# Normalisation factors held one per token on partitions, and the rotations of the grouped heads at another place

## The reference, cut to what matters

```python
def rmsnorm(x, g):
    y = xf * lax.rsqrt(jnp.mean(xf * xf, axis=-1, keepdims=True) + NORM_EPS)
    return (y * g).astype(x.dtype)
...
        x_gq = rope2d(rmsnorm(x_gq, gqa_q_norm_g[i]))
        x_gk = rope2d(rmsnorm(x_gk, gqa_k_norm_g[i]))
...
    s = jnp.einsum('bqhgd,bkhd->bhgqk', qblk, k) * scale
    p = jax.nn.softmax(s, axis=-1)
...
    od = (o1 - lam * o2)[:, :, :, 0, :]
    od = rmsnorm(od, subln_g) * (1.0 - lambda_init)
    og = attend(gq.reshape(B, S, GQA_KV_HEADS, GQA_GROUP, HEAD_DIM), gk, gv)
    o = jnp.concatenate([od.reshape(B, S, DIFF_WIDTH), og.reshape(B, S, GQA_WIDTH)], axis=-1)
    return o @ w_out
```

## Time and profile before

| | |
|---|---|
| median of 3 runs | 1671.21 us (1670.35 to 1672.07) |
| span of the profiled execution | 1662.7 us |
| time around the span, by the median | 8.5 us |
| PE, DVE, ACT, POOL busy | 84%, 57%, 37%, 18% of the span |
| moved by DMA | 572 MB, 344 GB/s in the mean |
| stage of the projections | about 37 to 143 us |
| attention and output of the first tile | about 143 to 196 us |
| expert loop with the gathers | from about 214 us |

### The profile page before, as it was taken

One profiled execution on the slowest core, in us unless ns is written; L12 is line 12 of the kernel. 1 busy time (PEld: TensorE's weight loads), 2 busy tenths in 40 slices (PEclk: granted clock), 3 DMA queues, 4 the chain that ended last, 5 costly groups with the idle time before them and its releaser, 6 DMA issues.

```text
span 1662.7 us, 21762 instructions
## 1 busy us (share of the span) xinstructions
PE 1397.3 (84%) x8112; PEld 860.6 (52%) x8112; DVE 951.8 (57%) x2127; ACT 623.5 (37%) x1464; POOL 300.1 (18%) x277
## 2 busy tenths in 40 slices
PE   5997877777776666677676999999999999999997
PEld 4884744543432323233322899898745454545443
DVE  4989588666668677677765788675431212121213
ACT  3334558354445444344443337544421111111111
POOL 0000034334435443444441000000000000000000
PEclk8999999989999888888977999999999999999999
DMA  9772189999999999999998534343799999999996
GB/s 395 283 270 97 39 346 398 395 427 418 417 427 413 421 426 399 427 423 425 427 424 339 193 133 150 123 178 136 316 385 427 426 427 427 428 427 427 426 427 273
DMA packets 80015, 572.09 MB, mean 344 GB/s; under 512 B 9136, under 2 KB 9392, under 8 KB 11184
## 3 DMA queue, kind: packets, MB, share of 16 engines
q1 hardware_dynamic: 40608, 284.55, 42.1%
q0 software_dynamic: 39312, 286.28, 41.8%
HBM read 569.75 MB, written 1.05 MB: 343 GB/s over the span
## 4 chain that ended last, share of the span: by engine, by line
PE 48%; DMA 17%; DVE 14%; SPq 11%; ACT 5%; issue 3%; POOL 1%; POOLq 0%; DVEq 0%; ACTq 0%
DMA big<-in_peer_dram,misc 13%; PE bank L1889 11%; SPq L518 11%; PE bank L1454 7%; DVE big L2241 5%; PE bank L1678 4%; PE bank L1399 2%; PE bank L1876 2%; PE bank L1636 2%; PE bank L1640 2%; DMA big<-in_moe_far_up_dram 2%; PE bank L1632 1%; POOL big L626 1%; DMA ring<-in_first_dram 1%; PE bank L1208 1%
## 5 line engine op out<-in xcount | busy, mean ns | idle before, releaser
L1454 PE MATMUL bank<-big 128*64 128x512 f32 x1024 | 302.4, 720 | 190.6 <-ACT big L821 189.9
L626 POOL DMA_INDIRECT big<-in_peer_dram,misc x256 | 290.7, 1135 | 472.6 <-PE bank L1454 338.2
L1454 PEld LDWEIGHTS bank<-big 128*64 128x64 f32 x1024 | 70.3, 153 | 352.8 <-ACT big L821 245.3
L2241 DVE SCALAR_TENSOR_TENSOR big<-big 128x1024 f32<-128x1024 f32 x128 | 156.0, 1226 | 98.9 <-DMA big<-in_peer_dram,misc 98.0
L2241 DVE SCALAR_TENSOR_TENSOR big<-big,misc 128x1024 f32<-128x1024 f32 x128 | 155.3, 1224 | 77.3 <-DMA big<-in_peer_dram,misc 76.2
L815 ACT ACTIVATE misc<-misc 128x1 f32<-128x1 f32 x256 | 51.5, 201 | 265.0 <-DVE big L2241 252.7
L1889 PE MATMUL bank<-big 128*64 128x512 f32 x640 | 140.2, 593 | 4.0 <-DMA big<-in_moe_far_up_dram 2.6
L2678 DVE SCALAR_TENSOR_TENSOR big_parts<-bank,misc,big_parts 128x512 fp32r<-128x512 f32 x32 | 22.5, 746 | 160.1 <-ACT big_parts L1099 160.1
L2668 DVE TENSOR_TENSOR misc<-misc,bank 128x512 f32<-128x512 f32 x16 | 11.0, 689 | 164.3 <-PE bank L1889 164.3
L1889 PEld LDWEIGHTS bank<-big 128*64 128x64 f32 x640 | 45.8, 137 | 95.8 <-issue 89.3
L821 ACT ACTIVATE big<-misc 128x64 f32<-128x64 f32 x256 | 89.0, 348 | 8.4
(11 more groups left out here) (485 smaller groups left out, 2574.0 us busy)
## 6 DMA issues: line engine op xcount, KB each, us to landing
big<-in_moe_down_dram SPq DMA_DIRECT2D x40, 1024.0 KB, 23.6
big<-in_moe_gate_dram SPq DMA_DIRECT2D x40, 1024.0 KB, 25.3
ring<-in_second_dram SPq DMA_DIRECT2D x36, 1024.0 KB
ring<-in_first_dram SPq DMA_DIRECT2D x33, 1024.0 KB
big<-in_moe_far_up_dram SPq DMA_DIRECT2D x20, 1024.0 KB, 22.6
big<-in_moe_up_dram SPq DMA_DIRECT2D x20, 1024.0 KB, 21.0
misc<-in_mod_rest_dram POOLq DMA_DIRECT2D x16, 1024.0 KB, 5.2
ring<-in_moe_gate_dram SPq DMA_DIRECT2D x12, 1024.0 KB, 21.5
```

The costliest lines, as they stand in the source:

```text
L626: pool.indirect_dma_start(out=gathered[b % GATHERS], out_offset=None, in_=t["peer"], in_offset=bass.IndirectOffsetOnAxis(ap=rows[:, b % 32 ...
L1454: last = nc.tensor.matmul(bank[2 * tt + half][HALF * g:HALF * (g + 1), :], diag[:, b % DIAGS, :], gathered[b % GATHERS][:, a:a + 512], sta ...
L2241: dve.scalar_tensor_tensor(u, u, 1.0, x_pairs[b // (BLOCKS // 2)][:, b % 2, :], ALU.mult, ALU.mult, accum_out=dots[:, b % 32:b % 32 + 1]). ...
```

## The change

The factors of the three norms are no longer spread over 128 x 512 elements, but held with tokens on partitions.

- **Grouped queries.** ACT squares a unit straight from PSUM and then copies it with the gain as scale. The sum over a head is eight products with the squares as the stationary operand and two columns of ones moving, the result 16 columns. The root is of the sum plus 64 times epsilon, which folds the factor of the scores' scale in. The inverse isn't multiplied into the queries: it is the scale of the exponential and a factor of the negative maximum. Queries are rotated without it.
- **Grouped keys.** Four products give sums per token (8 columns), then root and inverse; eight products of the inverse, repeated over 64 columns, with the identity spread it over bank 6, and DVE multiplies from PSUM.
- **Differential heads.** Four products with one column, root and inverse of 4 columns; then spread_od, four products with the identity, and DVE multiplies from PSUM. In out_first the fourth column block isn't begun early any more, and the blocks' banks change places.
- **Order.** The key sum stands after gq0 and not after gq1; the spread after gq2, behind a wait for the inverse; the query sums and the rotations of gk, gq0 and gq1 after gv; those of gq2 and gq3 after dv0. On DVE the rotations stand before pairs 10 and 11 instead of behind all pairs, and the multiplication of the keys behind remainder 9.

```diff
-        csT = small[:, 24:40]
+        eps_head = small[:, 1:2]
+        head_inv = small[:, 24:40].rearrange("p (t u r) -> p t u r", t=TT, u=4)
+        key_inv = small[:, 106:114].rearrange("p (t r) -> p t r", r=2)
+        od_inv = small[:, 114:118]
...
-            return bank[((0, 1, 4, 6), (2, 3, 5, 6))[tt][n % 4]][:, 0:P]
+            return bank[((1, 4, 6, 0), (2, 3, 5, 6))[tt][n % 4]][:, 0:P]
...
-                act.activation(dst[what](i), src, ACT.Copy).then_inc(S("win_taken"), 1)
+                if what == "gq":
+                    act.activation(sq[:, 2 + i // 2, (i % 2) * T:(i % 2 + 1) * T], src, ACT.Square).then_inc(S("sqg_ready"), 1)
+                    act.activation(dst[what](i), src, ACT.Copy, scale=v("gq_g")).then_inc(S("win_taken"), 1)
+                else:
+                    act.activation(dst[what](i), src, ACT.Copy).then_inc(S("win_taken"), 1)
...
-                if what == "gq":
-                    act.wait_ge(S("win_taken"), n + 1)
-                    act.activation(sq[:, 2 + i // 2, (i % 2) * T:(i % 2 + 1) * T], gqT[:, i, :], ACT.Square).then_inc(S("sqg_ready"), 1)
-                if n in (11, 14, 15):
-
-                    j = (11, 14, 15).index(n)
-                    act.wait_ge(S("ssg_ready"), base("ssg_ready") + j + 1)
-                    act.activation((rsk, rsg[:, 0:512], rsg[:, 512:1024])[j], bank[6][:], ACT.Sqrt, scale=1.0 / HD,
+                if n == 10:
+                    act.wait_ge(S("ssg_ready"), base("ssg_ready") + 1)
+                    act.activation(key_inv.rearrange("p t r -> p (t r)"), bank[6][:, 0:8], ACT.Sqrt, scale=1.0 / HD,
                                    bias=eps).then_inc(S("stdg_ready"), 1)
+                if n == 14:
+                    act.wait_ge(S("ssg_ready"), base("ssg_ready") + 2)
+                    act.activation(head_inv.rearrange("p t u r -> p (t u r)"), bank[6][:, 0:16], ACT.Sqrt, scale=1.0,
+                                   bias=eps_head).then_inc(S("stdg_ready"), 1)
...
+            def score_scale(i, r):
+                tt, t_, gqa = item(i)
+                return head_inv[:, tt, t_, r:r + 1] if gqa else HD ** -0.5
...
-                    act.activation(Pb[:, slot, r, :], bank[score_bank(i, r)][:], ACT.Exp, scale=HD ** -0.5,
+                    act.activation(Pb[:, slot, r, :], bank[score_bank(i, r)][:], ACT.Exp, scale=score_scale(i, r),
...
-                act.activation(rs_od, bank[0][:], ACT.Sqrt, scale=1.0 / P, bias=eps).then_inc(S("stdo_ready"), 1)
+                act.activation(od_inv, bank[0][:, 0:4], ACT.Sqrt, scale=1.0 / P, bias=eps).then_inc(S("stdo_ready"), 1)
...
+            head_sums = halves.rearrange("p (r c) -> p r c", r=2)[:, :, 0]
...
+                if n_win == 10:
                     pe.wait_ge(S("sqg_ready"), base("sqg_ready") + 1)
-                    nc.tensor.matmul(bank[6][:], halves, sq[:, 0, :], start=True, stop=True).then_inc(S("ssg_ready"), 1)
-                if n_win in (14, 15):
-                    g = n_win - 14
-                    pe.wait_ge(S("sqg_ready"), base("sqg_ready") + 3 + 2 * g)
-                    pe.wait_ge(S("stdg_ready"), base("stdg_ready") + 1 + g)
-                    nc.tensor.matmul(bank[6][:], halves, sq[:, 2 + g, :], start=True, stop=True).then_inc(S("ssg_ready"), 1)
+                    for tt in range(4):
+                        last = nc.tensor.matmul(bank[6][:, 2 * tt:2 * tt + 2], sq[:, 0, tt * P:(tt + 1) * P], head_sums, start=True, stop=True)
+                    last.then_inc(S("ssg_ready"), 1)
+                if n_win == 12:
+                    pe.wait_ge(S("key_inverse"), 1)
+                    for tt in range(4):
+                        for r in range(2):
+                            last = nc.tensor.matmul(bank[6][HD * r:HD * (r + 1), tt * P:(tt + 1) * P], key_inv[:, tt, r:r + 1].broadcast_to([P, HD]), ident,
+                                                    start=True, stop=True)
+                    last.then_inc(S("key_spread"), 1)
+                if n_win == 14:
+                    pe.wait_ge(S("sqg_ready"), base("sqg_ready") + 5)
+                    pe.wait_ge(S("gk_normed"), base("gk_normed") + 1)
+                    for tt in range(TT):
+                        for u in range(4):
+                            a = (u % 2) * T + tt * P
+                            last = nc.tensor.matmul(bank[6][:, 8 * tt + 2 * u:8 * tt + 2 * u + 2], sq[:, 2 + u // 2, a:a + P], head_sums,
+                                                    start=True, stop=True)
+                    last.then_inc(S("ssg_ready"), 1)
+                    rope_mm([gkT[:, T:]])
+                    pe.wait_ge(S("win_taken"), 13)
+                    rope_mm([gqT[:, 0, :], gqT[:, 1, :]])
                 if n_win == 13:
                     sum_rest(0)
                 if n_win == 15:
                     turn_rest(0)
-                if n_win == 16:
-                    pe.wait_ge(S("gk_normed"), base("gk_normed") + 1)
-                    rope_mm([gkT[:, T:]])
-            for j in range(2):
-                pe.wait_ge(S("gq_normed"), base("gq_normed") + j + 1)
-                rope_mm([gqT[:, 2 * j, :], gqT[:, 2 * j + 1, :]])
...
-                nc.tensor.matmul(bank[0][:], ones, sqo, start=True, stop=True).then_inc(S("sso_ready"), 1)
+                for h in range(4):
+                    last = nc.tensor.matmul(bank[0][:, h:h + 1], sqo[:, h * P:(h + 1) * P], ones[:, 0:1], start=True, stop=True)
+                last.then_inc(S("sso_ready"), 1)
+
+            def spread_od(tt):
+                pe.wait_ge(S("od_inverse"), tt + 1)
+                for h in range(4):
+                    last = nc.tensor.matmul(bank[2 * tt][:, h * P:(h + 1) * P], od_inv[:, h:h + 1].broadcast_to([P, P]), ident, start=True, stop=True)
+                last.then_inc(S("od_spread"), 1)
...
-                for n in range(4):
+                for n in range(3):
                     if n % 2 == 0:
                         pair_landed(pe, (OUT0 + n) // 2)
                     part(n, order[:4])
+                    if n == 0:
+                        spread_od(0)
...
-                    part(n, order[4:] if n < 4 else order).then_inc(S("out0_done"), 1)
+                    part(n, order[4:] if n < 3 else order).then_inc(S("out0_done"), 1)
...
+                if (s, q) == (1, 4):
+                    spread_od(1)
...
-            link(dve.reciprocal(rsk, rsk))
-            dve.scalar_tensor_tensor(gkT, gkT, v("gk_g"), rsk, ALU.mult, ALU.mult).then_inc(S("gk_normed"), 1)
+            dve.reciprocal(key_inv, key_inv).then_inc(S("key_inverse"), 1)
             rest_in(9)
-            for _ in range(2):
-                mod_pair()
+            dve.wait_ge(S("key_spread"), 1)
+            dve.scalar_tensor_tensor(gkT, gkT, v("gk_g"), bank[6][:], ALU.mult, ALU.mult).then_inc(S("gk_normed"), 1)
+            mod_pair()
+            dve.wait_ge(S("gk_normed"), base("gk_normed") + 1)
+            rope(gkT[:, T:].unsqueeze(1), 1)
+            rope(gqT[:, 0:2, :], 2)
             rest_in(10)
-            for _ in range(4):
-                mod_pair()
+            mod_pair()
+            rope(gqT[:, 2:4, :], 2)
+            mod_pair()
 
             def take_rest(half):
 
                                          three(v("b_mod", 16 + 16 * half, 16), 4), ALU.add)
 
             take_rest(0).then_inc(S("rest_taken"), 1)
-            for j in range(2):
-                dve.wait_ge(S("stdg_ready"), base("stdg_ready") + 2 + j)
-                link(dve.reciprocal(rsg[:, j * 512:(j + 1) * 512], rsg[:, j * 512:(j + 1) * 512]))
-                dve.scalar_tensor_tensor(gqT[:, 2 * j:2 * j + 2, :], gqT[:, 2 * j:2 * j + 2, :], v("gq_g"),
-                                         three(rsg[:, j * 512:(j + 1) * 512], 2), ALU.mult, ALU.mult).then_inc(S("gq_normed"), 1)
-            mod_pair()
-            dve.wait_ge(S("gk_normed"), base("gk_normed") + 1)
-            rope(gkT[:, T:].unsqueeze(1), 1)
-            dve.wait_ge(S("gq_normed"), base("gq_normed") + 2)
-            for j in range(2):
-                rope(gqT[:, 2 * j:2 * j + 2, :], 2)
-
+            dve.wait_ge(S("stdg_ready"), base("stdg_ready") + 2)
+            link(dve.reciprocal(head_inv, head_inv))
...
-                    dve.tensor_scalar(nmx[:, c:c + 1], mx[:, c:c + 1], -HD ** -0.5, None, ALU.mult).then_inc(S("nmax_ready"), 1)
+                    tt, t_, gqa = item(i)
+                    if gqa:
+                        dve.tensor_scalar(nmx[:, c:c + 1], mx[:, c:c + 1], head_inv[:, tt, t_, r:r + 1], -1.0, ALU.mult, ALU.mult).then_inc(S("nmax_ready"), 1)
...
-            def normalise_od(tt):
+            def invert_od(tt):
                 name = ("stdo_ready", "stdo1_ready")[tt]
                 dve.wait_ge(S(name), base(name) + 1)
-                if tt == 0:
-                    for part in range(4):
-                        ins = dve.reciprocal(rs_od[:, part * P:(part + 1) * P], rs_od[:, part * P:(part + 1) * P])
```

(42 more changed lines are left out.)

6 lines of the change are left out of this document (3 added, 3 removed).

## The result

The changed kernel takes 1680.82 us (median of 6 executions, 1676.27 to 1688.59). The kernel before, timed beside it, takes 1671.97 (1670.35 to 1674.45). The ratio is 1.0058, with a 95% interval of 1.004 to 1.0076: **8.85 us slower**, where 2.9 slower were forecast. A second timing gave 1680.12 and a ratio of 1.0062 (1.004 to 1.0085).

What follows compares the result with a forecast made beforehand. DVE and its modulation pieces were taken to pace the projections, and DMA gathers the expert loop from 213 us. Entry +4.9, first tile 0 and loop -2.0 sum to +2.9: 1674.1 us, range 1669.5 to 1679.0.

Steps and rivals of the forecast that it cites:

- PE's pause behind the key inverse: First block's projections: PE stops after gq2 for DVE's small reciprocal, from 93.05 to 96.8, 3.75 us.
- clock at 0.50, work lost: Behind that PE stop: 3.4 us at half clock, 1.7 us of work lost, bounds 0 and 2.1.
- DVE's wait before the gk rotation: Projections: DVE idle from 102.9 to 113.1, 10.2 us, with pairs 10 to 15 queued behind.
- piece 13, issue to arrival: Modulation piece in the projections: 5.1 us alone, plus 1.2 for meeting SyncE's 1 MB ring load.
- piece 15: Last modulation piece in the projections: asked for at 137.0, arriving at 142.1.
- entry in all: First block's projections up to the first scores: +4.9 us, of which +4.4 to scores(0) and +0.5 half clock.
- first tile's output: Output product of the first token tile: 0, ScalarE's wait covering the later start; +1.0 without that cover.
- expert loop, blocks 0 to 32: Second tile's norm: reciprocal gone from the chain, transfer regained, -2.0 us, bounds 0 and -2.5.
- around the span: Time outside the profiled span: 8.5 us, the median 1671.21 less the span, taken as unchanged.
- B: Rival, neither clock nor sharing: entry costs +1.5, loop gives -0.5, 1670.7 us; chance 0.26.
- C: Rival: the loop gives nothing back, PE being the limit, and piece 13 pays 2.5: +6.2, 1677.4 us; chance 0.22.
- D: Rival: second tile's reciprocal repaid in full, 3.2 plus 1.7 of half clock: -3.4, 1667.8 us; chance 0.10.

Runs made afterwards that it cites:

- after: The changed kernel as first measured and profiled, against the kernel before: 1680.82 us, ratio 1.0058.
- ring_late: Changed kernel with SyncE's ring pairs 19 and 20 held until all modulation pairs are done: 1674.41 us, ratio 1.0035 to the kernel before.
- after_again: The changed kernel run again, unaltered: 1680.12 us, ratio 1.0062 to the kernel before.
- loads_late: Changed kernel with ring pairs 19 and 20 and POOL's subkeys held until all modulation pairs are done: 1672.96 us, ratio 1.0023 to the kernel before.
- pause_filled: Changed kernel with 16 unused products in PE's pause before the key inverse: 1676.9 us, ratio 1.005 to the kernel before.
- od_only: Kernel before with only the differential heads' factors per token, projections as before: 1668.35 us, ratio 0.9991 to the kernel before.
- pairs_first: Changed kernel with pairs 10, 11 and remainder 10 before DVE's gk rotation wait, pair 12 between rotations: 1666.29 us, ratio 0.998 to the kernel before.
- spread_later: Changed kernel with the key spread moved behind gq3 and sum_rest(0): 1673.74 us, ratio 1.0036 to the kernel before.
- pe_kept_busy: Changed kernel with 48 unused products on PE between dv3 and sum_rest(1): 1680.55 us, ratio 1.0063 to the kernel before.
- before_again: The kernel before, unaltered, executed once for a second profile: span 1666.0 us, device time 1667.88 us.

## Why the prediction was wrong

The direction, the added wait and the list of what turns up late were right; the sum was 6 us short, and most of it is one step. The measured walk beside the predicted one:

| step of the prediction | predicted | measured in after |
|---|---|---|
| PE's pause behind the key inverse | 3.75 | 3.75 |
| clock at 0.50, work lost | 3.4, 1.7 | 6.6, of which 1.8 within the pause; 2.4 (half of 4.84 busy) |
| DVE's wait before the gk rotation | 10.2 | 11.27 |
| piece 13, issue to arrival | 6.3 | 8.75 |
| piece 15 | 5.1 | 7.86 |
| sum_rest(1) to first maximum | 3.7 | 3.97 |
| entry in all | +4.9 | +11.1 |
| first tile's output | 0 | 0.0 (19.63 us both) |
| expert loop, blocks 0 to 32 | -2.0 | -0.9 against the second profile, +0.3 against the first |
| around the span | 8.5 | 1.8 |

**The step that failed: the two pieces.** From the dk rotation to sum_rest(1) the walk was 5.9 us short: 2.5 for piece 13, 2.8 for piece 15, and 0.65 for what lies ahead of them (the wait on DVE was 1.07 longer, the work around it 0.4 shorter). For piece 13 I saw the ring load of the same instant and took 1.2 us, half of an upper bound of 2.5. No row gives that bound (it is what 1 MB takes at the 427 GB/s of the earlier trace rows): the subkeys of the earlier trace rows, which I named for it, took 8.4 where I had 5.0 to 5.25, so 3.2 to 3.4 more, and piece 13 paid 3.3 (8.75 less the 5.45 of ring_late). The row had the size, and I took a third of it. For piece 15 I took 5.1, as if it were alone: I hadn't followed SyncE's next pair, which the end of dv3 releases, nor the early load behind it. That ring_late alone brings the two pieces to 5.45 and 5.41 shows the cause. The 5.1 was a little low besides: with the ring held they took 5.18 to 5.46.

The Trainium skill, "DMA: Bandwidth & Descriptors", "Rules for kernel authors", on transfers of different engines that interleave, was taken in the prediction as even sharing, an estimate of 2.5 us for piece 13. The trace agrees that they delay each other, but the 3.3 goes beyond that estimate. Nor was it even: the ring load issued with the piece landed in 5.1 us in after and in 4.8 in after_again, and the one issued at 113.5, with nothing beside it, took 5.1. So here the piece paid for both. The fit of the same page ("Anatomy of one DMA", for loads that POOL issues), an estimate of 4.4 us for 1 MB, was too low by 0.6 to 1.1: pieces with no load of SyncE's beside them took 5.02 to 5.46 (loads_late).

**The clock** was a term of the right kind and a small miss. The rival without it (B) falls: pause_filled shows 2.3 us of DVE's wait. That a pause of 3.75 cost more half-clock time than one of 2.89 I couldn't read from the rows. Nor is the length of a pause enough to tell: 2.35 us before 283.62 left the clock at 1.00 in the earlier trace rows, but in od_only the same pause, 2.34 us at the same step (287.61), came with 3.4 us at 0.50, from 287.35 to 290.76. These runs don't show what decides. PE's timeline of od_only and its window:

```profile
287.61 3.49 PE L1467 MATMUL bank<-big 128*64 128x512 f32 x8 [2.34 <-ACT big L822]
...
287.35:290.76 3.41, 3.15 (x8) 1.00 (x10) 3.31 (x8) 3.17 (x5) 0.00 (x0) 0.50 1.01 425
```

**The loop.** Blocks 16 to 32 gain what was argued: 44.0 us against 46.3, with 411 GB/s where the earlier trace rows has 306 and the second profile of before 348 (by the working of the prediction 348 would have given 1.7 us, not 2.5). Blocks 0 to 16 lose: 48.5 against 47.1 and 46.0. A stretch at half clock lies at another step in after: in the second profile of before it began 11 us behind the first block's dot product, here it falls 20 us into the loop, and the transfers sink to 240 GB/s right behind it (the windows above). PE's timeline of after, and of the second profile of before:

```profile
254.04 3.59 PE L1487 MATMUL bank<-big 128*64 128x512 f32 x8 [2.73 <-ACT big L829]
```

```profile
233.79 3.42 PE L1454 MATMUL bank<-big 128*64 128x512 f32 x8 [3.21 <-ACT big L821]
```

That isn't what these blocks lose. In pairs_first the stretch begins 12 us behind the first block (233.45 less 221.2), as before the change, and blocks 0 to 16 still take 48.3:

```profile
233.45:236.86 3.41, 3.41 (x10) 0.75 (x6) 3.23 (x10) 3.38 (x7) 0.82 (x1) 0.50 1.01 428
```

Every kernel with the new part 1 shows 47.9 to 48.8, wherever the stretch lies, and od_only 47.3, like the second profile of before. So the 1 us or so comes with part 1; by what way stays open.

**Around the span.** I took the median less the span for what lies around it. That was the difference between two executions. It did the forecast no harm, since the sum of the steps was in effect added to the median, but a reader of the 8.5 would look for work that isn't there.

**The rivals.** C had the sign and a piece that pays 2.5, and came nearest with 1677.4, in part by luck: it had no second piece. That the loop gives nothing back in sum isn't ruled out (-0.9 or +0.3 by the profiles; od_only -1.0, with an interval that takes in zero), but its reason is: the transfers run at 389 to 411 GB/s with the extra spread on PE. D, the loop repaid in full, fell: it gained 1 us at most, not 4.9. That the factors alone, in the old order, give -6.5 was no rival of mine; I had priced them only inside the new order.

## What to carry to other kernels

Separate an arithmetic saving from the reordering that comes with it: here the first gained 6.5 us and the second cost 17. When an engine that issues or consumes double-buffered transfers is made to wait, everything behind it starts later, so walk the other queues to the new instant too, and charge a waited-for transfer with all that starts beside it, at the size that your own rows show. Take a second profile of the kernel before where its execution may have been a quick one; a distance between two events inside the trace is safer than an absolute time.

## What the runs showed of the hardware

- Two loads of 1 MB issued together can delay each other by more than half, and who pays isn't fixed. In after SyncE's landed in 5.1 us and POOL's in 8.75, where it took 5.45 with the ring held; spread_later and pe_kept_busy repeat it (5.0 and 8.76; 4.8 and 8.70). In pause_filled, issued 0.06 us apart as well, they took 7.70 and 8.28, in pairs_first at 113.4 us 7.87 and 8.94. Where SyncE's came 1.4 us behind a piece (before_again, 122.18), it took 6.29 and the piece 5.22.
- Subkeys issued 0.5 us behind a piece on the same queue delayed it by 0.2 us at most: 5.41 with them, 5.18 without. They landed themselves only after 7.4 us.
- The clock's low stretch around a short pause wasn't of one length: 3.4 us with 2.89 us of idle PE, 6.6 with 3.75. A pause of 2.35 us left the clock at 1.00 in one execution of before, one of 2.34 at the same step came with 3.4 us at 0.50 in od_only. Filling the pause of 3.75 with products kept it at 1.00.
- The same kernel before took 55.6 us from the dk rotation to the first maximum in two executions, while the stretch ahead of that differed by 2.3 us, with a granted clock of 0.88 and 0.78 from 30 to 60 us.
